# The triangular inverse of a gated DeltaNet: 16x16 diagonal blocks solved on VectorE lanes instead of by three matmul levels

## The reference

```python
    kk = jnp.einsum('bhnid,bhnjd->bhnij', k, k)
    A = jnp.where(strict, beta[..., :, None] * kk * decay, 0.0)
    T = lax.linalg.triangular_solve(eye + A, jnp.broadcast_to(eye, A.shape),
                                    left_side=True, lower=True, unit_diagonal=True)
    u = jnp.einsum('bhnij,bhnjd->bhnid', T, beta[..., None] * v)
    w = jnp.einsum('bhnij,bhnjd->bhnid', T, (beta * jnp.exp(G))[..., None] * k)
    ...
    def step(S, xs):
        v_new = u_c - jnp.einsum('bhcd,bhde->bhce', w_c, S)
        o = jnp.einsum('bhcd,bhde->bhce', qg_c, S) + jnp.einsum('bhij,bhje->bhie', attn_c, v_new)
        S = S * jnp.exp(gl_c)[..., None, None] + jnp.einsum('bhcd,bhce->bhde', kd_c, v_new)
```

## Time and profile before

| | us |
|---|---|
| median of 3 runs | 1402.16 (1393.28 to 1403.96) |
| the profiled execution | 1391.07, its span 1389.3 |
| busy, of the span: PE, DVE, ACT, POOL | 88%, 54%, 41%, 9% |
| one turn of the head loop | 88.1 |
| mean granted TensorE clock | 0.946 |

### The profile page before, as it was taken

The page is one execution under the profiler, slowest core; times in us unless marked ns, Lnnn a source line. Parts: engine busy times, 40 slices in busy tenths (PEclk is TensorE's granted clock), DMA queues, the critical chain, the costliest instruction groups (busy, mean ns, idle before and its releaser), DMA issues.

```text
span 1389.3 us, 21355 instructions
## 1 busy us (share of the span) xinstructions
PE 1222.5 (88%) x8126; PEld 1081.2 (78%) x8126; DVE 756.8 (54%) x914; ACT 574.0 (41%) x756; POOL 123.0 (9%) x164
## 2 busy tenths in 40 slices
PE   5989999999999999999989999961888988988870
PEld 4989999999999999999989999961555555555540
DVE  4436365463653645536465544245676666677635
ACT  5424233342332423323332322251666666666632
POOL 0012030020300203003020000004000000000002
PEclk9999999999999999999999999985899999999995
DMA  5272121222212112122112234625889889988836
GB/s 190 89 228 79 64 86 47 82 66 77 83 47 81 66 62 79 60 73 81 63 36 76 91 125 163 236 101 195 324 307 330 329 305 330 327 318 327 328 105 221
DMA packets 50680, 218.06 MB, mean 157 GB/s; under 512 B 6064, under 2 KB 8720, under 8 KB 38352
## 3 DMA queue, kind: packets, MB, share of 16 engines
q1 hardware_dynamic: 41200, 194.05, 40.0%
q0 software_dynamic: 4080, 15.30, 3.1%
q10 hardware_dynamic: 5360, 8.17, 1.7%
HBM read 186.49 MB, written 31.00 MB: 157 GB/s over the span
## 4 chain that ended last, share of the span: by engine, by line
PE 75%; DVE 7%; ACT 7%; DMA 4%; issue 4%; POOL 1%; ACTq 1%; SPq 0%; DVEq 0%; POOLq 0%
PE proj L616 25%; PE proj L1348 15%; PE wideB L1369 7%; PE proj L998 5%; PE wideB L382 4%; PE proj L941 3%; PE wideA L388 3%; PE wideA L1335 2%; DVE xbl L1437 2%; ACT xbh L1433 2%; PE small L998 2%; DMA wraw<-in_w_in 2%; PE wideB L395 1%; PE gram L365 1%; POOL scr_rows L1796 1%
## 5 line engine op out<-in xcount | busy, mean ns | idle before, releaser
L616 PE MATMUL proj<-xnh,whi 128*128 128x288 f32 x1152 | 349.4, 303 | 12.2 <-DVE xnl L1883 6.6
L616 PE MATMUL proj<-xnh,wlo 128*128 128x288 f32 x1152 | 348.2, 302 | 0.0
L616 PE MATMUL proj<-xnl,whi 128*128 128x288 f32 x1152 | 346.6, 301 | 0.0
L616 PEld LDWEIGHTS proj<-xnh,whi 128*128 128x128 f32 x1152 | 218.6, 190 | 13.5 <-issue 5.9
L1425 DVE TENSOR_TENSOR elo<-eraw,ehi 128x4096 fp32r<-128x4096 f32 x64 | 214.6, 3354 | 20.6 <-ACT ehi L1415 20.5
L616 PEld LDWEIGHTS proj<-xnl,whi 128*128 128x128 f32 x1152 | 218.5, 190 | 0.0
L616 PEld LDWEIGHTS proj<-xnh,wlo 128*128 128x128 f32 x1152 | 218.3, 190 | 0.2
L1348 PE MATMUL proj<-ehi,xbh 128*80 128x512 f32 x256 | 111.5, 436 | 34.0 <-DVE xbl L1437 34.0
L628 DVE TENSOR_TENSOR wlo<-wraw,whi 128x1024 fp32r<-128x1024 f32 x72 | 92.7, 1287 | 66.3 <-ACT whi L624 66.3
L1415 ACT ACTIVATE ehi<-eraw 128x4096 fp32r<-128x4096 f32 x32 | 116.0, 3626 | 1.3
L624 ACT ACTIVATE whi<-wraw 128x1024 fp32r<-128x1024 f32 x72 | 75.8, 1053 | 87.6 <-PE proj L616 69.3
(11 more groups left out here) (315 smaller groups left out, 2213.7 us busy)
## 6 DMA issues: line engine op xcount, KB each, us to landing
wraw<-in_w_in SPq DMA_DIRECT2D x72, 512.0 KB, 3.3
eraw<-in_w_gate SPq DMA_DIRECT2D x32, 1024.0 KB, 4.9
eraw<-in_w_up SPq DMA_DIRECT2D x32, 1024.0 KB, 7.4
eraw<-in_w_down SPq DMA_DIRECT2D x32, 1024.0 KB, 5.6
wraw<-in_w_out SPq DMA_DIRECT2D x24, 512.0 KB, 3.5
xb<-scr_rows SPq DMA_DIRECT2D x32, 320.0 KB, 5.9
scr_y<-yout SPq DMA_DIRECT2D x32, 320.0 KB, 5.7
grow<-scr_row POOLq DMA_DIRECT2D x8, 640.0 KB, 4.3
```

What stands on the lines that cost most here:

```text
L616: mm = pe.matmul(out, w[:, kc, :], x[:, kc, hh * HALF:(hh + 1) * HALF], start=(j == 0), stop=(j == 23))
```

## The change

Of the seven doubling steps (the first by mask, six levels) three levels remain. The 16x16 diagonal blocks, 8 in each of 5 units, become 40 lanes of VectorE: the queue stores `aT` to DRAM (`scr_a`) and reads the diagonal blocks back as `ablk`, 40 partitions x 16 x 16; `solved_row` computes row after row of all 40 inverses (15 rows, each a product and a sum); ScalarE turns the blocks round into a second tile; both go to the diagonals of two zeroed DRAM matrices (`scr_t`), and these are loaded whole into `TT` and `T`. The solve stands at positions 11 to 15, the levels start at position 22, the scan at 31, and what follows moves with it, the last steps with one or two positions more between them. In the three levels only the 64 columns of each unit that matter are computed. The DMAs are issued from the SP queue after the loads of weight tiles 6, 7 and 8. Two zero stores are added in head 0, and the queue waits for all four before the loop.

```diff
-LEVELS = 6
+LEVELS = 3
+BASE = 16
+LANES = P // BASE * UNITS
...
+        def diagonal(matrix):
+            return bass.AP(matrix.tensor, 0, [[BASE * P + BASE, LANES], [P, BASE], [1, BASE]])
+        def unit_blocks(matrix):
+            return bass.AP(matrix.tensor, 0, [[P, P], [P * P + P, UNITS], [1, P]])
...
-        LEVEL0 = 10
+        LEVEL0 = 22
+        SOLVE0 = 11
...
-            if p == 8:
-                pe.wait_ge(s["tt_set0"], n)
-                for u in range(UNITS):
-                    mm = pe.transpose(wideA[:, U[u]], TT[:, U[u]], ident)
-                mm.then_inc(s["t_turned0"], 1)
...
                     if k == 0:
-                        pe.wait_ge(s["t_set0"], n)
+                        pe.wait_ge(s["t_in"], 16 * n)
+                        pe.wait_ge(s["tt_in"], 16 * n)
...
-                        mm = pe.matmul(wideB[:, U[u]], aT[:, U[u]], T[:, U[u]], start=True, stop=True)
+                        mm = pe.matmul(wideB[:, H[u]], aT[:, U[u]], even(T[:, U[u]], k), start=True, stop=True)
...
-            if p == 8:
-                act.wait_ge(s["t_turned0"], n)
-                act.activation(T[:, :], wideA[:, 0:UW], ACT.Copy).then_inc(s["t_set0"], 1)
+            if p == SOLVE0 + 5:
+                act.wait_ge(s["row_sum"], (BASE - 1) * n)
+                wait(act, s["t_out"], 16 * g)
+                act.activation(lanes(tblk[1]), tblk[0][0:LANES, :, :].rearrange("l c i -> l i c"), ACT.Copy)\
+                   .then_inc(s["blk_turned"], 1)
...
+        def solved_row(dve, row, g):
+            done = (BASE - 1) * g + row
+            wait(dve, s["row_sum"], done - 1)
+            dve.scalar_tensor_tensor(prod[0:LANES, 0:row, 0:row],
+                                     ablk[0:LANES, 0:row, row].unsqueeze(1).to_broadcast([LANES, row, row]), -1.0,
+                                     tblk[0][0:LANES, 0:row, 0:row], ALU.mult, ALU.mult).then_inc(s["row_mul"], 1)
+            dve.wait_ge(s["row_mul"], done)
+            dve.tensor_reduce(tblk[0][0:LANES, 0:row, row], prod[0:LANES, 0:row, 0:row], X, ALU.add)\
+               .then_inc(s["row_sum"], 1)
+        def blocks_out(sp, g):
+            n = g + 1
+            sp.wait_ge(s["a_set"], n)
+            sp.dma_start(unit_blocks(scr_a), units(aT[:, :])).then_inc(s["a_out"], 16)
+            sp.wait_ge(s["a_out"], 16 * n)
+            sp.dma_start(lanes(ablk), diagonal(scr_a)).then_inc(s["a_in"], 16)
+        def blocks_back(sp, g):
+            n = g + 1
+            sp.wait_ge(s["row_sum"], (BASE - 1) * n)
+            wait(sp, s["kv_done"], 4 * g)
+            sp.dma_start(diagonal(scr_t[0]), lanes(tblk[0])).then_inc(s["tt_out"], 16)
+            sp.wait_ge(s["blk_turned"], n)
+            sp.dma_start(diagonal(scr_t[1]), lanes(tblk[1])).then_inc(s["t_out"], 16)
+        def inverse_in(sp, g):
+            n = g + 1
+            sp.wait_ge(s["tt_out"], 16 * n)
+            sp.dma_start(units(TT[:, :]), unit_blocks(scr_t[0])).then_inc(s["tt_in"], 16)
+            sp.wait_ge(s["t_out"], 16 * n)
+            sp.dma_start(units(T[:, :]), unit_blocks(scr_t[1])).then_inc(s["t_in"], 16)
+        SP_AT = {6: blocks_out, 7: blocks_back, 8: inverse_in}
...
-                dve.tensor_tensor(units(TT[:, :]), units(aT[:, :]), first_mask, ALU.mult).then_inc(s["t_cut"], 1)
...
+            if SOLVE0 <= p < SOLVE0 + 5:
+                if p == SOLVE0:
+                    dve.wait_ge(s["a_in"], 16 * n)
+                    wait(dve, s["tt_out"], 16 * g)
+                for row in range(3 * (p - SOLVE0) + 1, 3 * (p - SOLVE0) + 4):
+                    solved_row(dve, row, g)
...
+            sp.dma_start(lanes(tblk[0]), A["eyes"]).then_inc(par_in, 16)
...
+            for k in range(2):
+                sp.dma_start(scr_t[k], zero[:, 0:UNITS * (P + 1)]).then_inc(zero_out, 16)
+            sp.wait_ge(zero_out, 64)
             with sp.Fori(1, HEADS) as i:
                 for t in range(TILES):
                     tile_load(i, t)
+                    if t in SP_AT:
+                        SP_AT[t](sp, i - 1)
...
-            with sp.Fori(1, KC // 2) as j:
-                for k in range(2):
-                    out_load(2 * j + k, k)
-                    gate_load(2 * j + k, 0, k, gate)
+            for q in range(2, KC):
+                out_load(q, q % 2)
+                gate_load(q, 0, q % 2, gate)
+                if q + 4 in SP_AT:
+                    SP_AT[q + 4](sp, HEADS - 1)
```

More of the change, by code:

```diff
@@ L124, in level_mask, with lanes @@
         def level_mask(k, count=UNITS):
-            c = C_LEVEL + P * k
-            return const[:, c:c + P].unsqueeze(1).to_broadcast([P, count, P])
+            c = C_LEVEL + HP * k
+            return const[:, c:c + HP].unsqueeze(1).to_broadcast([P, count, HP])
+        def diagonal(matrix):
+            return bass.AP(matrix.tensor, 0, [[BASE * P + BASE, LANES], [P, BASE], [1, BASE]])
+        def unit_blocks(matrix):
+            return bass.AP(matrix.tensor, 0, [[P, P], [P * P + P, UNITS], [1, P]])
+        def lanes(t):
+            return t[0:LANES, :, :]
         def level_units(k):
@@ L186, in encoder_layer @@
         TT = sb(gd, "TT", [P, UW])
-        cut = sb(gd, "cut", [P, UW])
+        cut = sb(gd, "cut", [P, UNITS * HP])
+        ablk = sb(gd, "ablk", [P, BASE, BASE])
+        tblk = [sb(gd, f"tblk{k}", [P, BASE, BASE]) for k in range(2)]
+        prod = sb(gd, "prod", [P, BASE - 1, BASE - 1])
         vr = sb(gd, "vr", [P, UW])
@@ L323, in units, with halves, even @@
             return ap.rearrange("p (u m) -> p u m", m=P)
+        H = [slice(u * HP, (u + 1) * HP) for u in range(UNITS)]
+        def halves(ap):
+            return ap.rearrange("p (u m) -> p u m", m=HP)
+        def even(ap, k):
+            return ap.rearrange("p (q two b) -> p q two b", two=2, b=BASE << k)[:, :, 0, :]
         ST_Q, ST_K, ST_KEPS, ST_RK2, ST_NORM, ST_BRK, ST_QEPS, ST_O, ST_TOT, ST_ROOT, ST_OREC = range(0, 55, 5)
-        LEVEL0 = 10
+        LEVEL0 = 22
+        SOLVE0 = 11
         SCAN0 = LEVEL0 + 3 * LEVELS
@@ L519, in gdn_vector @@
                     dve.wait_ge(s["tat_done"], done + 1)
-                    into = T if k < LAST else TT
-                    dve.tensor_tensor(into[:, 0:w], into[:, 0:w], wideA[:, 0:w], ALU.add).then_inc(s["t_set"], 1)
+                    if k < LAST:
+                        into, add = even(T[:, :], k), wideA[:, 0:w].rearrange("p (q b) -> p q b", b=BASE << k)
+                    else:
+                        into, add = units(TT[:, 0:2 * w])[0:HP, :, HP:P], halves(wideA[0:HP, 0:w])
+                    dve.tensor_tensor(into, into, add, ALU.add).then_inc(s["t_set"], 1)
             c, step = chunk_at(p)
@@ L1887, in _ @@
             split_low(dve, 0, 1)
+            dve.wait_ge(par_in, 16 * 4)
             dve.wait_ge(ba_w, 1)
@@ L1948, in constants @@
     i, j = np.arange(P)[:, None], np.arange(P)[None, :]
-    parts = [i == j, i <= j, None, np.ones((P, P)), i < j]
-    for k in range(LEVELS + 1):
-        b = 2 ** k
-        cut = (i // (2 * b) == j // (2 * b)) & ((i // b) % 2 == 1) & ((j // b) % 2 == 0)
-        parts.append(-cut.astype(np.float32))
-    parts[2] = parts[5].T
+    parts = [i == j, i <= j, np.ones((P, P)), i < j]
+    column = np.arange(HP)[None, :]
+    for k in range(LEVELS):
+        b = BASE << k
+        parts.append(-((i // (2 * b) == column // b) & ((i // b) % 2 == 1)).astype(np.float32))
     valid = np.ones((P, UNITS))
@@ L2006 @@
         "w_out": np.concatenate([tiles_of(w_out_a[0]), tiles_of(w_out_b[0]), tiles_of(w_o[0])], axis=0),
+        "eyes": np.broadcast_to(np.eye(BASE, dtype=np.float32), (LANES, BASE, BASE)),
         "state": np.asarray(state_gdn)[0, 0],
```

47 lines of the change are left out of this document (23 added, 24 removed).

## The result

The changed kernel takes 1448.69 us (median of 4 runs, 1444.28 to 1450.94), the kernel before beside it 1398.55 (4 runs, 1393.28 to 1403.96): ratio 1.036 with the interval 1.032 to 1.041. It is slower. The profiled execution is 1444.28 us long, its span 1442.6; against the 1391.07 of before that is +53.2 us, where the prediction's sum had +34. The medians differ by 50.1 us.

The account below looks back on a forecast made before the run. TensorE's work was taken to bound the head loop. Per head -11.3 + 12.4 + 3.0 = +4.1 us, +29 over seven; last head +1, start +4: +34 on 1391, 1425, taken as 1430; range 1385 to 1475.

Parts of the forecast that it names:

- Work taken away: TensorE, per head: three levels and first transposes 9.6 us, narrow last product 0.2, wait for `on` 1.5; 11.3 us less.
- Step 1: SP queue: the store of `aT`, ready at 464.5, is issued at 466.4, after the load of weight tile 6.
- Step 2: DRAM round trip: store of `aT` lands in 3.3 us, `ablk` comes in 2.4 us later, at 472.1.
- Step 3: VectorE solve of 30 dependent operations, 9.2 us, with a split and two convolution steps between: 11.8 us, to 483.9.
- high bound: Rival with dear small runs, chance 0.14: `ablk` 4.5 us, pitch 0.30, TT and T 1 us longer each; stall 19, 1471.
- Step 4: Loads of TT and T stand behind weight tile 8, which waits for the split of tile 5: 4.8 us, to 488.7.
- Step 5: Weight tile lands in 3.3 us, TT and T add 0.8 each: T is in at 493.6.
- wait: TensorE stands still at the first level for T and TT from DRAM, 12.4 us in each head.
- Slow clock: After its rest TensorE runs mostly at 1.2 GHz; 3.0 us charged per head.
- Start: Head 0 waits for all zero stores before weight tile 0 of head 1 is issued: +4 us.
- Last head: Beside the first output projection: five us for VectorE's gated sum, 2.5 at the first level, 3 slow clock, against 9.8: +1.
- the inverse comes nearly in time: Rival, chance 0.14: a stall at the first level below about 5.5 us makes the change faster by over 1%.

## Why the prediction was right, and where its sum was off

The forecast case came in: TensorE waits in each head for the DMA into T at the first level's A x T, and the kernel is slower by more than it saves. The sum was 19 us too low. Point by point, for the head walked (it starts 28.4 us later here, 492.91 standing for 464.5):

- **Work taken away**: 11.3 predicted, 13.0 by the run without the path. Taken from start to start in a middle head, before and without the path, the 1.7 us more have a place. From one A x T to the next it was 6.53, 6.26, then 6.16 us: two of the three levels that go are dearer than the one I priced, 0.5 us. The full levels that stay take 5.97 us and not 6.16, the last 4.87 and not 4.97: 0.5 us, of which my sum had 0.2. And from the scan to the next head's start 2.4 us are saved and not the 1.5 of the earlier trace rows. The cheaper full level does not come from narrow matmuls, since it is as cheap with wide ones (5.96); VectorE's cut in it is half as wide now (128x320), but no run takes that alone. The matmuls' narrow columns gave nothing, as I took from the earlier trace rows, and the narrow weights of the last product 0.1 us of a head and not 0.2.
- **Step 1**, the store's issue 1.9 us after `aT`: 494.86 - 492.91 = 1.95. Right.
- **Step 2**, the store at 3.3 us: this is the term that was mis-sized. It took 6.33 here, 6.1 in the median. I had priced it by the landing of a weight tile, 3.3, as though a transfer behind a tile only had to wait for it in part. Alone in its queue it takes 2.8, below what I charged; with the tile's 512 KB 0.4 us ahead of it 6.1, the sum of the two, and the tile lands late as well (5.8); VectorE's 6.24 us of idling, where I had forecast 3, are this term. `ablk`, 2.4 predicted, is in and used 2.34 us after its issue: right, with its 64 B runs. The small runs that one rival feared are cheap; on the ten engines that the Trainium skill gives such a transfer (DMA: Bandwidth & Descriptors, Why a DMA increments its semaphore by 16 and not by 1), no run here shows anything.
- **Step 3**, solve and what lies between: 11.8 predicted, 503.55 to 514.40 = 10.85. The first operations start 0.18 to 0.20 us apart on 40 lanes and not 0.22; 1.0 us better. With all 15 rows in one stretch the solve alone takes 8.9 us, 9.2 by my sum. The 0.30 us at which the high bound spaces two small ones no run shows.
- **Step 4**: 4.8 predicted, 514.40 to 519.01 = 4.6. Right, in its parts too: the silu, the high part, the low part.
- **Step 5**: 4.9 predicted from the split's end to T, 519.01 to 525.12 = 6.1. The same fault as in step 2: I counted TT and T beside a tile at 0.8 each.
- So the **wait** is 12.4 + 3.0 - 1.0 - 0.2 + 1.2 = 15.4 by these pieces, and 15.6 in the trace. TensorE reached the level 16.7 us after `aT`, as predicted.
- **Slow clock**: 3.0 charged by the earlier trace rows, which have a rest of 5.5 us. It was 4.6 on average: 95.1 - 75.0 - 15.5, the mean rest of the middle heads; the run with 112 matmuls gives 4.4 by another way. The fault was not that the rest was short, but to take one sample of a price that scatters. By the same difference single middle heads of the changed kernel paid 2.2 to 5.3 us for rests of 15.1 to 16.4, the run with the steps in order and the levels from 22 paid 5 for 5.3, and the one with TT and T ahead of tile 8 paid 2.6 for 11.3.
- Per middle head that is -13.0 + 15.5 + 4.6 = +7.1 and not +4.1; the 4.6 is the remainder, so this sum closes by itself, and only the 4.4 tests it. Over all seven turns it is +46 and not +29.
- **Start**: +4 predicted, +3.3 measured. The mechanism fits: with the wait for the zero stores moved, and the stores themselves still there, it is gone. But the start scatters by as much between profiles. **Last head**: +1 predicted, +4.0. The two waits come as forecast, 4.4 us for the gated sum (5 predicted) and 4.2 at the first level (2.5); half clock follows each of them, where I had counted it once.
- **No wait for `on`**: right.

Of the rivals, *the inverse comes nearly in time* is what the reordered kernels show and the changed one doesn't: only another order makes the path that short. The high bound had the right direction, a longer wait, but for a wrong reason: it put most of it on the small runs of `ablk` and the spacing of the solve, and it was the store behind the tile. The total came closer than its terms: 1.7 us more saved and 1.2 less in steps 3 and 4 hid part of the 4.2 more in steps 2 and 5 and of the 1.6 more for the clock.

## What to carry to other kernels

Price a new transfer by what is issued in the same queue just ahead of it, not by the transfer of the nearest size: between +3.6% and -5.3% lie here only the order of a few DMAs, of the solve's rows and of two activations, the place of one wait and a later start of the levels, with the same arithmetic. When a path is moved off the busiest engine, walk every in-order queue that it crosses, the innocent instructions behind each new wait too (an eviction, a silu), and give it as many positions as it takes plus what it pushes back. And a rest of TensorE costs more than its length: in these runs up to some 5 us on top, and how much did not follow from how long it rested.

## What the runs showed of the hardware that I had not expected

- A DRAM store of 320 KB: 2.8 us alone in its queue, 6.1 with a load of 512 KB issued 0.4 us before it, which itself then takes 5.8 us instead of 3.4. Two loads of 320 KB that follow such a tile: 4.4 and 4.9 us; without it 3.3 and 3.6, and the tile is hardly slower with them behind it (3.8).
- After a rest of 15.6 us TensorE's granted clock stayed at 0.50 for 10.5 us of unbroken work, after one of 15.1 in the same kernel for 4.3; after rests of 5.1 to 5.6 us for 10 to 11, after rests of about 11 for about 5; after rests of 2.8 and 3.0 us the half clock lasted 10.2 us in one head and 3.4 in another. Useless matmuls in the wait, up to its end, kept it at 1.00 and made the kernel about 22 us faster.
- Dependent VectorE operations on 40 lanes start 0.18 to 0.20 us apart while they have at most 9 elements a lane, and 0.24 at 36: a 16x16 triangular solve of 40 blocks, thirty such operations, takes 8.9 us, and less than 11 with two convolution steps and a split in between.
